# The outputs of the last two experts added to their tokens by TensorE with gate matrices, the other expert rows loaded and added beforehand, and the first experts' rows gathered in two halves

## The reference

```python
xf = rms_norm(h, norm_ffn[i])                      # 512 x 1024
p_group = softmax(xf @ wr_g + br_g)                # 4 groups, the best one is taken
pv, pi = top_k(softmax(expert logits of that group), 2)   # 2 of its 8 experts
gates = pg * pv / sum(pv)
for each expert e (32 of them), for the tokens that chose it:
    a, b = split(x @ w_gu[e], 2)                   # w_gu[e]: 1024 x 1024
    y = (silu(a) * b) @ w_down[e]                  # w_down[e]: 512 x 1024
h = h + segment_sum(y * gate, token)               # each token gets two rows
```

## Time and profile before

| | |
|---|---|
| runs | 2946.41, 2953.13, 2952.37 us; median 2952.37 |
| profiled execution | 2951.22 us, its span 2949.4 us, mean granted TensorE clock 0.970 |
| busy | PE 2712.5 us (92%), DVE 1147.1 (39%), ACT 640.2 (22%), POOL 287.2 (10%) |
| DMA | 609.63 MB, mean 207 GB/s |
| first expert layer | its products run from 438.16 to 975.3 us, its last addition ends at 997.3 us |
| second expert layer | its products run from 1530.25 to 2046.3 us, its last multiplication by the gain ends at 2076.1 us |

### The profile page before, as it was taken

One profiled execution on the slowest core, in us unless ns is written; L12 is line 12 of the kernel. 1 busy time (PEld: TensorE's weight loads), 2 busy tenths in 40 slices (PEclk: granted clock), 3 DMA queues, 4 the chain that ended last, 5 costly groups with the idle time before them and its releaser, 6 DMA issues.

```text
span 2949.4 us, 35284 instructions
## 1 busy us (share of the span) xinstructions
PE 2712.5 (92%) x14334; PEld 1765.6 (60%) x14334; DVE 1147.1 (39%) x2561; ACT 640.2 (22%) x1316; POOL 287.2 (10%) x278
## 2 busy tenths in 40 slices
PE   7999999999999699999999989997699998999998
PEld 5858763544444476776763434443577667865864
DVE  4344443112122544424342111111755455665566
ACT  2130421123222100000021010000353441043053
POOL 2002001111110000001000111110200001212211
PEclk9999999999999899999999999998899999999999
DMA  5604249999998522232369999997310211320310
GB/s 182 264 3 144 115 175 368 417 414 415 379 418 360 211 86 72 71 134 97 138 272 396 419 421 417 416 421 329 117 37 31 67 38 58 97 83 19 107 26 36
DMA packets 115068, 609.63 MB, mean 207 GB/s; under 512 B 13005, under 2 KB 25357, under 8 KB 88144
## 3 DMA queue, kind: packets, MB, share of 16 engines
q1 hardware_dynamic: 92000, 541.98, 46.1%
q0 software_dynamic: 20224, 54.17, 5.4%
q10 hardware_dynamic: 2672, 11.09, 1.0%
HBM read 587.79 MB, written 35.65 MB: 211 GB/s over the span
## 4 chain that ended last, share of the span: by engine, by line
PE 74%; DMA 11%; DVE 6%; PEld 3%; issue 2%; ACT 2%; PEldq 0%; SPq 0%; DVEq 0%; POOLq 0%; ACTq 0%; POOL 0%
PE psum L689 24%; PE psum L2206 11%; DMA ring<-in_expert_w_gu 7%; PE psum L2218 6%; PE psum L818 6%; PE psum L944 5%; PE psum L589 4%; DMA arena<-in_expert_w_gu 3%; PE psum L973 3%; PE psum L962 3%; PE psum L579 2%; PE psum L1241 2%; PEld psum L689 2%; PE psum L1266 1%; PE psum L2199 1%
## 5 line engine op out<-in xcount | busy, mean ns | idle before, releaser
L2206 PE MATMUL psum<-ring,XT 128*64 128x512 f32 x1024 | 242.1, 613 | 21.5 <-DMA ring<-in_expert_w_gu 19.6
L2206 PE MATMUL psum<-arena,XT 128*64 128x512 f32 x1024 | 240.1, 612 | 15.2 <-DMA arena<-in_expert_w_gu 14.9
L2278 DVE TENSOR_TENSOR XT<-XT,psum 64x512 f32<-64x512 f32 x64 | 44.1, 690 | 513.2 <-ACT XT L2281 513.2
L689 PE MATMUL psum<-arena 128*128 128x256 f32 x1056 | 238.7, 379 | 0.0
L689 PEld LDWEIGHTS psum<-arena 128*128 128x128 f32 x1056 | 200.3, 190 | 27.1
L944 PE MATMUL psum<-arena 64*128 64x384 f32 (+7 forms) x736 | 187.7, 474 | 27.5 <-ACT arena L998 16.6
L689 PE MATMUL psum<-XT,ring 128*128 128x256 f32 x864 | 195.3, 380 | 5.3 <-DVEq L3284 5.3
L689 PEld LDWEIGHTS psum<-XT,ring 128*128 128x128 f32 x864 | 163.3, 190 | 32.3 <-issue 6.8
L2206 PEld LDWEIGHTS psum<-ring,XT 128*64 128x64 f32 x1024 | 76.4, 140 | 163.8 <-issue 127.6
L818 PE MATMUL psum<-ring,arena 128*128 128x512 f32 x384 | 166.6, 593 | 4.4 <-DVEq L3284 2.0
L2206 PEld LDWEIGHTS psum<-arena,XT 128*64 128x64 f32 x1024 | 76.6, 140 | 156.1 <-issue 132.4
(11 more groups left out here) (386 smaller groups left out, 3834.0 us busy)
## 6 DMA issues: line engine op xcount, KB each, us to landing
ring<-in_expert_w_gu SPq DMA_DIRECT2D x64, 2048.0 KB, 19.6
arena<-in_expert_w_gu SPq DMA_DIRECT2D x64, 2048.0 KB, 20.1
arena<-in_expert_w_down SPq DMA_DIRECT2D x32, 2048.0 KB, 13.6
ring<-in_expert_w_down SPq DMA_DIRECT2D x32, 2048.0 KB, 12.4
ring<-in_ada_w SPq DMA_DIRECT2D x12, 2048.0 KB, 8.0
ring<-in_fox_w_in SPq DMA_DIRECT2D x8, 2048.0 KB, 12.5
ring<-in_ret_w_in SPq DMA_DIRECT2D x8, 2048.0 KB, 9.7
ring<-in_c_in_w SPq DMA_DIRECT2D x8, 2048.0 KB, 7.7
```

What stands on the lines that cost most here:

```text
L689: m = pe.matmul(ps[0][:, 2 * P * i:2 * P * (i + 1)], x, w, start=(not onto and i == 0 and c == 0), stop=(c == 3), skip_group_check=True)
L2206: i = pe.matmul(psum[side * BR:(side + 1) * BR, 0:FF], x[:, 4 * part + c, :], w[:, c, side * FF:(side + 1) * FF], start=(part == 0 and c = ...
```

## The change

For the last two experts (`LATE = 2`, experts 30 and 31) nothing is stored to `y_dram`. `down_late` puts expert 30 on partitions 0 to 63 and expert 31 on 64 to 127 of two PSUM banks, one for each half of the 1024 columns. A matrix `S` holds, for each token, its gate at the slot of its row in expert 30 or 31; `place_late` makes it (DVE), `turn_late` turns it (PE), `lay_late` copies it (DVE). `weigh_late` multiplies it with the rows (PE) and `late_sum` adds the product to `H` (DVE, from PSUM). The 1024 rows in `y_dram` are loaded by SP once the stores of experts 28 and 29 have landed and expert 30's `up` has ended, and added by DVE right after its last work for expert 31, with gates that are zero for rows of the last two experts (and for overflow rows). So that unwritten rows are finite, `y_dram` is cleared at the kernel's start and the gather buffers on POOL before the first gather.

In routing, `first_rows` reads contiguous slices of `H`, the weights of experts 0 and 1 are loaded in the matching order, the last two token tiles are done in two halves of the columns, and DVE takes each half by itself. ACT loads the table of Silu at the routing stage's end.

```diff
 # RouteProj
-                pool.wait_ge(*self.n("lists", 1))
+                pool.wait_ge(*self.n("listed", 1))
+                pool.memset(XT[...][:, 0:2 * D], 0.0).then_inc(self.r("lists"), 1)
+                pool.wait_ge(*self.n("lists", 2))
...
-                self.first_rows(pe, 0, 0, 2)
+                self.first_rows(pe, 0, 0, 3)
                 self.turn(pe, NT - 1)
-                self.first_rows(pe, 0, 2, 5)
+                self.first_rows(pe, 0, 3, 6)
                 self.logits(pe, NT - 1)
...
-                self.first_rows(pe, 2, 0, KC)
-                self.first_rows(pe, 3, 0, KC).then_inc(self.experts.s("turned"), 1)
+                for c0, signal in ((0, self.r("first_half")), (4, self.experts.s("turned"))):
+                    self.first_rows(pe, 2, c0, c0 + 4)
+                    self.first_rows(pe, 3, c0, c0 + 4).then_inc(signal, 1)
                 self.table(pe, 1)
...
-                    i = pe.matmul(psum[...], H[:, t, c::KC],
+                    i = pe.matmul(psum[...], H[:, t, c * P:(c + 1) * P],
...
                 act.activation(rt[:, 9, 20:24], rt[:, 9, 12:16], ACT.Exp).then_inc(self.r("exps"), 1)
+                act.activation(rt[:, 9, 40:41], cols[:, 0:1], ACT.Silu)
...
 # overflow: seven more small DVE steps for LATE_GATE, OVER_GATES and EARLY_GATES
 # Experts, SP, behind all weight loads
-                    src = self.dn[e] if what == 2 else self.gu[e, :, 4 * what:4 * what + 4, :]
+                    src = self.dn[e] if what == 2 else (self.gu if e > 1 else self.gu_kp)[e, :, 4 * what:4 * what + 4, :]
...
+                sp.wait_ge(*self.used(3 * (NE - LATE) + 1))
+                for e in (NE - LATE - 2, NE - LATE - 1):
+                    sp.wait_ge(*self.stored(e))
+                for t in range(NT):
+                    sp.dma_start(self.YG[:, t, :, :], rows[:, t, :, :]).then_inc(self.s(f"got{t}"), 16)
...
 # Experts, PE
+            def down_late(self, pe, e, w):
+                rows = slice((e + LATE - NE) * BR, (e + LATE - NE + 1) * BR)
+                for c in range(4):
+                    for half in range(2):
+                        i = pe.matmul(bank(self.LATE_BANKS[half])[rows, :], self.HT[:, c, :],
+                                      w[:, c, half * BANK:(half + 1) * BANK], start=(c == 0), stop=(c == 3))
...
+                    if e == NE - LATE:
+                        self.turn_late(pe)
+                n = pe.value_load(ovn[0:1, 0:1], min_val=0, max_val=EXTRA)
                 down(NE - 1)
-                n = pe.value_load(ovn[0:1, 0:1], min_val=0, max_val=EXTRA)
                 with pe.If(n > 0):
...
+                self.weigh_late(pe)
+            def turn_late(self, pe):
+                for t in range(NT):
+                    i = pe.transpose(bank(3)[:, t * P:(t + 1) * P], self.ST[:, t]..., ident)
+            def weigh_late(self, pe):
+                for t in range(NT):
+                    for half in range(2):
+                        if t == 0:
+                            pe.wait_ge(self.s("y"), self.at("y") + NE - LATE + half + 1)
+                        i = pe.matmul(bank(self.SUMS[t] + half), self.S[:, t * P:(t + 1) * P], self.Y[half], start=True, stop=True)
+                    i.then_inc(self.s("late_weighed"), 1)
 # Experts, DVE
+            def collect_early(self, dve):
+                for t in range(NT):
+                    dve.wait_ge(self.s(f"got{t}"), self.at(f"got{t}") + 16)
+                    for k in range(2):
+                        i = dve.scalar_tensor_tensor(H[:, t, :], self.YG[:, t, k, :], self.route.EARLY_GATES[:, k, t:t + 1], H[:, t, :],
+                                                     ALU.mult, ALU.add)
+            def late_sum(self, dve, t):
+                dve.wait_ge(self.s("late_weighed"), self.at("late_weighed") + t + 1)
+                return dve.tensor_tensor(H[:, t, :], psum[:, self.SUMS[t] * BANK:(self.SUMS[t] + 2) * BANK], H[:, t, :], ALU.add)
...
 # Experts, ACT: copies both banks to Y after the last down; POOL: no store for experts 30 and 31
 # Combine: no waits for the expert stage's end on PE, DVE, ACT (slack), no loads of its own;
 # per tile late_sum takes the place of the two gated additions
-                act.dma_start(self.G, io["norm_final"].partition_broadcast(P)).then_inc(self.s("gain"), 16)
+                    act.dma_start(HC[:, 0, :], io["norm_final"].partition_broadcast(P)).then_inc(sem("second_gain"), 16)   # during expert 16
 # start of the kernel: y_dram is cleared whole, 4 MB more
-(y_dram, 2 * SEQ // BR, 2 * SEQ // BR + EXTRA)
+(y_dram, 0, 2 * SEQ // BR + EXTRA)
```

More of the change, by code:

```diff
@@ L1172, in build @@
             each = dict(loaded=64, weighted=1, turned=2 * NT, taken=NT, taken_v=1, squared=NT, rstd=2, rowed=NT, logits=2, mask=2,
-                        ranked=2, counted=1, chosen=2, listed=1, lists=1, tops=1, exps=1, extra=1, kept=16 * 2, first=2)
+                        ranked=2, counted=1, chosen=2, listed=1, lists=2, tops=1, exps=1, extra=1, kept=16 * 2, first=2, first_half=1, half_taken=1)
             def r(self, name):
@@ L2233, in down @@
                     if e:
-                        pe.wait_ge(self.s("y"), self.at("y") + e)
-                    self.down(pe, self.weights(3 * e + 2)).then_inc(self.s("downed"), 1)
+                        pe.wait_ge(self.s("y"), self.at("y") + min(e, NE - LATE))
+                    if e == NE - LATE:
+                        pe.wait_ge(self.s("late_laid"), self.at("late_laid") + 1)
+                    w = self.weights(3 * e + 2)
+                    (self.down(pe, w) if e < NE - LATE else self.down_late(pe, e, w)).then_inc(self.s("downed"), 1)
                 for e in range(NE):
-                    if e % 2 == 0:
-                        pe.wait_ge(self.s("xt"), self.at("xt") + e // 2 + 1)
+                    if e == 0:
+                        pe.wait_ge(*self.route.n("half_taken", 1))
                     for half in range(2):
+                        if e % 2 == 0 and (e or half):
+                            pe.wait_ge(self.s("xt"), self.at("xt") + e // 2 + 1)
                         self.ready(pe, 3 * e + half)
@@ new lines, in lay_late @@
+            def lay_late(self, dve):
+                dve.wait_ge(self.s("late_turned"), self.at("late_turned") + 1)
+                dve.tensor_copy(self.S, bank(3)).then_inc(self.s("late_laid"), 1)
+            def collect_early(self, dve):
+                for t in range(NT):
+                    dve.wait_ge(self.s(f"got{t}"), self.at(f"got{t}") + 16)
+                    for k in range(2):
+                        i = dve.scalar_tensor_tensor(H[:, t, :], self.YG[:, t, k, :], self.route.EARLY_GATES[:, k, t:t + 1], H[:, t, :],
+                                                     ALU.mult, ALU.add)
+                        if k == 0:
+                            dve_step.then(dve, i)
+                i.then_inc(self.s("early"), 1)
@@ L2326, in act @@
                 n = act.value_load(ovn[0:1, 0:1], min_val=0, max_val=EXTRA)
-                result(NE - 1)
+                act.wait_ge(self.s("downed"), self.at("downed") + NE)
+                for half in range(2):
+                    act.wait_ge(*self.stored(NE - LATE - 2 + half))
+                    act.activation(self.Y[half], bank(self.LATE_BANKS[half]), ACT.Copy).then_inc(self.s("y"), 1)
                 self.lane.finished(act)
-                for e in (NE - 2, NE - 1):
-                    act.wait_ge(*self.stored(e))
                 with act.If(n > 0):
@@ L2421, in dve @@
                 for t in range(NT):
-                    dve.wait_ge(self.s(f"got{t}"), self.at(f"got{t}") + 16)
-                    for k in range(2):
-                        i = dve.scalar_tensor_tensor(H[:, t, :], self.YG[:, t, k, :], gates[:, k, t:t + 1], H[:, t, :], ALU.mult, ALU.add)
-                        if k == 0:
-                            dve_step.then(dve, i)
-                    i.then_inc(self.s("summed"), 1)
+                    self.experts.late_sum(dve, t).then_inc(self.s("summed"), 1)
                 for g in range(2):
@@ L2479, in dve @@
             def dve(self, dve):
-                dve.wait_ge(self.s("gain"), 16)
+                dve.wait_ge(sem("second_gain"), 16)
                 for t in range(NT):
-                    dve.wait_ge(self.s(f"got{t}"), self.at(f"got{t}") + 16)
-                    for k in range(2):
-                        i = dve.scalar_tensor_tensor(H[:, t, :], self.YG[:, t, k, :], gates[:, k, t:t + 1], H[:, t, :], ALU.mult, ALU.add)
-                        if k == 0:
-                            dve_step.then(dve, i)
-                    i.then_inc(self.s("summed"), 1)
+                    self.experts.late_sum(dve, t).then_inc(self.s("summed"), 1)
                     dve.wait_ge(*self.till("summed", t + 1))
@@ L2532, in ds @@
             def ds(self, name):
-                return sem(f"decay{self.half}_{name}")
+                return sem(f"decay_{name}")
             def sp(self, sp):
```

(4 more changed lines are left out.)

118 lines of the change are left out of this document (80 added, 38 removed).

## The result

The changed kernel takes 2922.1 us (median of 6 runs, 2920.6 to 2928.1) where the kernel before took 2952.2 beside it: a ratio of 0.990, 95% interval 0.9884 to 0.9915, that is 30.1 us less. Its profiled execution took 2920.6 us, with a span of 2918.8 us and a mean granted clock of 0.982.

The account below looks back on a forecast made before the run. Expert stages were taken as bound by weight transfers, with serial chains at their starts and ends. Gains 9.3 + 7.6 + 6.1 + 9.7 = 32.7 us off 2951.2 gave 2918.5, a median of 2919.5; range 2909 to 2937.

Parts of the forecast that it names:

- The end of the first layer: Last down, combining and additions in layer one: early loads and additions end it at 991.2 instead of 997.3, gain 6.1 us.
- The end of the second: Same chain in layer two, with multiplications by the gain: ends at 2066.4 instead of 2076.1, gain 9.7 us.
- The head: Routing stage with experts 0 and 1: gain 9.3 us in the first layer, 7.6 in the second.
- expert 0: Expert 0's up, 8.80 us partly at half clock, now follows dense records: gain 1.6 us, at worst nothing.
- expert 1: First layer only: a shorter pause behind the table load removes expert 1's low clock, gain 1.7 us, at worst nothing.
- `overflow`: Seven small added DVE steps, 1.4 us, ahead of expert 1's hidden rows, mostly covered: 0.5 us lost, bounds 0 and 1.4.
- The 32 records: PE's first-rows records behind ranks(1): 5.2 us instead of 7.93 with contiguous operands, gain 2.7, bounds 0.9 and 4.5.
- The halves: Between first rows and expert 0's up, DVE takes one half while PE makes the second: gain 0.9 us.
- The carry: The start's gain passes through the DMA-bound expert stages at full size, as the weight stream begins earlier with the same length.
- not carried: Rival: weights set the expert stages' ends regardless, only 15.8 us are left, 2936.5 us; chance 0.12.
- The branch: Rival: PE's overflow branch ahead of weigh_late enters the chain, costing 3.5 and 2.6 us, 2925.5 us; chance 0.08.
- Slower: Rival: stored-row loads queue behind waits on SP and land 25 us late in each layer, 2958 us; chance 0.03.

Follow-up runs that it names:

- the paired kernel: The changed kernel with each late expert's two down halves written to different 64 partitions, gates exchanged to match; 2919.9 us.
- the kernel without the call ahead: The changed kernel without Silu called once ahead, so its table load stands before expert 0's Silu again; 2927.1 us.
- end alone: The changed kernel with the routing start's part undone (strided operands, whole first rows, no Silu ahead, old weight order); 2938.2 us.
- the strided kernel: The changed kernel with every eighth element as stationary operand again in the first rows, halves and Silu ahead kept; 2929.9 us.
- start alone: The kernel before with only the routing start's part: contiguous operands, second pair in halves, Silu ahead, matching weight order; 2939.1 us.
- the kernel with the late loads: The changed kernel with the four loads of stored rows issued only after the last down; 2952.7 us.

## Why the prediction was right, point by point

It said 2919.5 us, and the median is 2922.1. (By its own working, 2918.5 and 1.2, it should read 2919.7.) Its sum was 32.7, its four places gave 30.9 and 30.4.

*The end of the first layer*: predicted 6.1, measured 6.1. Late `down` took 7.0 where 6.9 was worked out from full-width records. The loads went out at 960.7 and the first landed 4.8 us later, DVE went on from its last step with no gap, and the last sum waited for PE. *The end of the second*: 9.7, measured 9.6, with DVE as the bound. That products to the same 64 partitions lose their partner is shown by the paired kernel, 7.05 against 3.65. The Trainium skill (TensorE: Matmul & The Clock Gate, Part 3: Packing small matmuls) says that the output's start partition is the column tile of the array and that matmuls in different tiles run concurrently. The trace agrees.

*The head*: 9.3 in the first layer, measured 8.5; 7.6 in the second, measured 6.6 and 6.1. By its terms in the first layer: ranks and mask 1.6 (1.6), expert 0 1.6 (1.7), table load 1.3 (1.3), expert 1 1.7 (2.0), `overflow` 0.5 lost (0.2 lost). Two terms were mis-sized. The 32 records were to gain 2.7 and gained 1.6: I let the clock be low for 3.3 us, and it was low for the first 5.1; where it was low for 3.4 (the kernel without the call ahead) they took 5.47 against the 5.2 of the prediction. The halves were to gain 0.9 and gained 0.4, because 0.5 us between `table(1)` and the next stage's first product is PE's own queue, which no view of before set apart. And one term had the right size for a reason that the runs do not bear out: expert 0's `up` was to gain because it follows dense records, but it took 7.09 us behind the strided ones too, in end alone and in the strided kernel. Expert 1's term, the low clock behind the table load, holds in the first layer, for which it was given.

*The carry.* Of some 15 us from the heads the middles gave back 2.4 to 4.5, where the prediction had put this at nothing. `turn_late` is 0.6 and 0.4 of it. In the second layer start alone shows another 0.9, so the stage bound by DMA does take some. The rival "not carried" is wrong in the main.

*The branch.* It did not come into the chain, as predicted, but the reason given was wrong: it was to take the 4.1 us of the earlier trace rows, begun 2 us into `down(31)`. It began with `down(31)` and took 7.0, since the change itself had put transfers beside it, the loads and behind them the next stage's weights. In the first layer it ended 0.07 us behind the last product (in the second 0.5 ahead of it), and once `down` was made faster it came into the chain at once. So this rival was nearer than its 0.08, and that it stayed out is luck: the slower `down` happened to cover it. The rule that I weighed against it (Runtime: NRT & Kernel Launch, Instruction fetch mechanics, in the Trainium skill) says that the sequencer fetches blocks of 16 KiB through a DMA queue of its own; the packet of 0.02 MB agrees.

*Slower*: it did not happen, the first tile landing where it was forecast. But the kernel with the late loads shows the mechanism, and at its price: its first tiles were 19.7 and 18.4 us later than forecast (counted from expert 31's Silu); by the prediction's 12 and 14 us that makes the ends 7.7 and 4.4 us longer than before, and they were 8.6 and 5.5 longer.

The total is thus closer than its parts, and that is luck: heads and carry were too hopeful by 4.6 to 6.3 us, and 3.5 to 5.1 us came back in pieces that the change hardly touches and the prediction did not count.

## What to carry to other kernels

When transfers are moved beside other work, look at the instruction fetches too: here a branch over a long block waited for a DMA of its own, and beside full DMA engines it took 5.9 to 7.3 us instead of 3.3 to 4.1. Queue enough products ahead of it. A short wait of PE can cost more than its length, because the records behind it may run at half clock. Before totals are compared, two numbers should be taken from every profile, the piece's own length and the clock in it, since one and the same kernel differed by 2 us in its first middle between two executions. Moving work off the last chain can be worth paying for on the engine that becomes free: here 6.8 us of slower products in each layer stood against 15.7 us won at the two ends. The paired kernel shows that even this price need not be paid, once something covers the branch.

## What the runs showed of the hardware

- The branch's time depends on the DMA engines: 3.3 to 4.1 us with a DMA share of 0.02 to 0.27, 5.9 to 7.3 us at 1.0, over the same block. Its instruction packet starts 0.9 to 1.1 us into it in the first case, 3.4 to 4.8 us in the second, and it ends 1.4 to 1.6 us behind the packet in both.
- A record of 128x128 by 128x128 with a stationary float32 operand of every eighth element takes 0.24 us at either clock; with a contiguous one 0.12 at full and 0.21 at half (24 records in the first 5.1 us of the changed kernel's 32). The Trainium skill (SBUF — State Buffer, Door 1: The DMA port swizzle) gives SBUF lines of 16 bytes, so that four float32 is the farthest stride that is free. The stride here is eight, and the trace agrees that it is not free.
- PE paused for 1.50 and 1.27 us ahead of the 32 records, and they began with 5.1 us at half clock. With products of no use in the two pauses the granted clock was 1.00 through all 32, in four stages of four; without them in one of eighteen.
- Half clock was also granted in a stretch where PE was 95% busy: 17 us from 139 us on in one execution, none there in another, with the same instructions.
- The first of the four loads of stored rows landed 4.7 us after its issue in the kernel before, and 7.6 us in the kernel with the late loads, beside a 1 MB store on another queue (both in the first layer).
